# A hybrid decoder step on one core: first layer's result turned where it is made, low-rank rows from unmixed rows, second low-rank maps inside the dense loop, shared buffers

## The reference, cut to what matters

```
x_prev = rows shifted by one;  xx = x_prev - x;  xm = x + xx * mu      # six mixes: w a r k v g
r, k, v, g = [xr, xk, xv, xg] @ w_in[j]
w_log = -softplus(-(w0 + tanh(xw @ w1) @ w2)) - 0.5                   # w1: 1024x64, w2: 64x1024
decay = exp(-exp(w_log));   a = sigmoid(a0 + (xa @ a1) @ a2)
kk = k * k_k, normalised per head;   k = k * (1 + (a - 1) * k_a)
per token and head:  S = S * w + sa (kk * a)^T + v k^T;   o = S r      # 16 heads of 64x64
out = (groupnorm(o) + bonus) * silu(g);   y = LayerNorm(ALPHA * x1 + out @ w_out)
```

## Time and profile before

| | us |
|---|---|
| median of the runs | 2200.3 |
| profiled execution, its own time | 2204.67 |
| its span, first to last instruction | 2202.9 |
| PE busy / DVE busy / ACT busy / POOL busy | 1834.0 / 1237.6 / 576.1 / 401.4 |
| phase_gate_out | 880.2 to 1095.4 |
| phase_rwkv_in before its loop | 1095.4 to 1199.3 |
| its dense loop | 1199.3 to 1497.8 |
| its value, gate and inverse part | 1497.8 to 1780.2 |
| phase_wkv | 1780.2 to 2026.8 |
| phase_out | 2026.8 to 2202.9 |

### The profile page before, as it was taken

One profiled execution on the slowest core, in us unless ns is written; L12 is line 12 of the kernel. 1 busy time (PEld: TensorE's weight loads), 2 busy tenths in 40 slices (PEclk: granted clock), 3 DMA queues, 4 the chain that ended last, 5 costly groups with the idle time before them and its releaser, 6 DMA issues. The chain is left out here.

```text
span 2202.9 us, 30628 instructions
## 1 busy us (share of the span) xinstructions
PE 1834.0 (83%) x11638; PEld 1063.8 (48%) x11638; DVE 1237.6 (56%) x2382; ACT 576.1 (26%) x1153; POOL 401.4 (18%) x376
## 2 busy tenths in 40 slices
PE   8999466899993998799747999978989957774887
PEld 4445234444442687447233666653454436563432
DVE  2000064888998765473467667677534335563584
ACT  0000004500012553121145555561121114341100
POOL 0001110000013554110000333320003312323110
PEclk9999688999996999798877999988979978896999
DMA  4100724212301100831164344434757284863811
GB/s 179 72 34 33 190 92 137 77 38 72 115 34 71 37 21 10 322 113 44 57 134 173 106 140 143 145 122 98 137 130 152 82 211 118 205 152 94 265 68 39
DMA packets 276576, 245.65 MB, mean 112 GB/s; under 512 B 131996, under 2 KB 229308, under 8 KB 276172
## 3 DMA queue, kind: packets, MB, share of 16 engines
q1 hardware_dynamic: 272420, 232.64, 36.9%
q0 software_dynamic: 2976, 9.02, 1.2%
q10 hardware_dynamic: 1040, 2.10, 0.4%
HBM read 161.60 MB, written 86.63 MB: 113 GB/s over the span
## 5 line engine op out<-in xcount | busy, mean ns | idle before, releaser
L555 PE MATMUL ix_ps<-ix_src,ei_xT 128*128 128x512 f32 x512 | 223.9, 600 | 9.4 <-DMA ix_src<-in_e_w_in 9.4
L1794 PE MATMUL ri_ps<-ri_xm,ri_w 128*128 128x384 f32 (+1 forms) x768 | 231.3, 455 | 0.1
L1890 PE MATMUL ri_ps<-ri_w,ri_xm 128*128 128x512 f32 x512 | 226.7, 605 | 0.0
L186 PE MATMUL ei_ps<-ei_w,ei_xT 128*128 128x512 f32 (+1 forms) x432 | 188.5, 598 | 3.9 <-DMA ei_w<-in_e_w_in 3.9
L1794 PEld LDWEIGHTS ri_ps<-ri_xm,ri_w 128*128 128x128 f32 x768 | 144.2, 190 | 73.0 <-issue 0.8
L633 DVE TENSOR_SCALAR_CACHE_REDUCE ix_flags<-score,ix_cand 128x384 bf16<-128x384 f32 (+1 forms) x186 | 163.7, 942 | 12.2 <-DVE ix_cand L650 12.0
L555 PEld LDWEIGHTS ix_ps<-ix_src,ei_xT 128*128 128x128 f32 x512 | 98.0, 192 | 132.7 <-issue 123.1
L1890 PEld LDWEIGHTS ri_ps<-ri_w,ri_xm 128*128 128x128 f32 x512 | 99.3, 195 | 124.5 <-issue 124.4
L1386 PE MATMUL co_psm<-co_w,co_srcT 128*128 128x512 f32 (+1 forms) x288 | 130.1, 611 | 11.6 <-DVE co_y L1436 10.8
L1112 PE MATMUL go_psm<-go_w,go_srcT 128*128 128x512 f32 (+1 forms) x288 | 135.1, 629 | 4.7 <-DVE go_y L1254 4.4
L186 PEld LDWEIGHTS ei_ps<-ei_w,ei_xT 128*128 128x128 f32 (+1 forms) x432 | 77.6, 181 | 114.0 <-issue 114.0
(11 more groups left out here) (328 smaller groups left out, 3037.9 us busy)
## 6 DMA issues: line engine op xcount, KB each, us to landing
ix_src<-in_e_w_in SPq DMA_DIRECT2D x4, 2048.0 KB, 11.2
scratch_h<-ix_stage SPq DMA_DIRECT2D x32, 256.0 KB
ri_w<-in_c_w_in SPq DMA_DIRECT2D x16, 512.0 KB, 5.5
ri_w<-in_c_w_in SPq DMA_DIRECT2D x4, 2048.0 KB, 9.3
ei_w<-in_e_w_in SPq DMA_DIRECT2D x3, 2048.0 KB, 19.9
scratch_h<-ei_stage POOLq DMA_DIRECT2D x24, 256.0 KB, 2.3
ix_src<-scratch_h SPq DMA_DIRECT2D x3, 2048.0 KB, 9.2
go_uvg<-scratch_h SPq DMA_DIRECT2D x8, 768.0 KB, 10.9
```

What stands on the lines that cost most here:

```text
L186: last = nc.tensor.matmul(ps[n % NB][0:rows(t), 0:cw], xT[:, kd, t * P:t * P + rows(t)], rhs, start=(kd == 0), stop=(kd == KD - 1))
L555: last = nc.tensor.matmul(ps[n % NB][:], xT[:, kd, t * P:(t + 1) * P], w_rest[s % 2][:, kd], start=(kd == 0), stop=(kd == KD - 1))
L1794: last = nc.tensor.matmul(out[:, 0:wd], w[:, ct % 2, kd, i * P:(i + 1) * P], xm[:, i, kd, lo:lo + wd], start=(kd == 0), stop=(kd == KD - 1))
L1890: last = nc.tensor.matmul(out[:], xm[:, j, kd, t * P:(t + 1) * P], w[:, a, kd], start=(kd == 0), stop=(kd == KD - 1))
```

## The change

1. phase_gate_out turns its own result: `result(t)` puts 8 transposes of each finished tile (L1120) and ACT copies (L1203) into the buffer `rows_T`, which phase_rwkv_in reads as x transposed. The sample rows' V cache has half the buffer: four sequences are loaded when the sample bias has been added, the other four once the first values are done.
2. phase_rwkv_in loads its parameters as rows and turns them (L1853). The two first low-rank weights are scaled twice, with 1-mu and with mu (L2219 on DVE), and the hidden rows are made from unmixed rows and rows shifted by one (L1865, L1870). The mixes w and a are not formed. All scaling by 1-mu is on ACT.
3. The second low-rank maps (L1883) and their Sigmoids (L2027) are inside the dense loop, one item ahead, straight into the buffer that the loop reads; the DRAM copies `e` and `a` are gone.
4. Buffers are shared by the odd layer's phases (`Shared`). The first keys, reads and the constants of phase_wkv are loaded in the last part of phase_rwkv_in, and w_out and three input tiles of phase_out during phase_wkv.
5. In phase_wkv the state update is one DVE sum (L2661), with the decayed state SP made ahead (L2665); the output buffer has three slots, and the group-norm steps stand at other hops.
6. In phase_out the sample transposes (L1417) stand between tiles, the sample steps come three tiles later, and on SP the exchange of their vectors stands ahead of the first store of y.

The diff, cut to its core:

```diff
+            def result(t):
+                m = rows(t)
+                pe.wait_ge(y_d, t + 1)
+                for hf in range(2):
+                    bank(hf, "y", t)
+                    for j in range(4):
+                        kd = hf * 4 + j
+                        last = nc.tensor.transpose(ps_t[hf][:, j * P:j * P + m], y[0:m, t % 2, kd * P:(kd + 1) * P], ident[0:m, 0:m])
+                    last.then_inc(tr[hf], 1)
...
-            for s in range(NT + 3):
+            for s in range(NT + 5):
                 if s == LAST + 2:
                     project(LAST, 0)
-                if s >= 2:
+                if 2 <= s <= LAST + 2:
                     project(s - 2, 1)
+                if s >= 4:
+                    result(s - 4)
...
+            def result(t):
+                m = rows(t)
+                at = 1 + t * P
+                for hf in range(2):
+                    act.wait_ge(tr[hf], count[hf]["y", t])
+                    nc.scalar.copy(rows_T[:, hf * 4:hf * 4 + 4, at:at + m],
+                                   ps_t[hf][:].rearrange("p (j n) -> p j n", j=4)[:, :, 0:m]).then_inc(turned[hf], 1)
...
-            def load_ea(x):
-                ct, q = item(x)
-                lo, wd = PIECES[q]
-                sp.wait_ge(lo_out[x % 2], 32 * (x // 2 + 1))
-                for i, n in enumerate(("e", "a")):
-                    sp.dma_start(ea[:, x % 3, i, 0:wd], g[n][ct * P:(ct + 1) * P, lo:lo + wd]).then_inc(ea_in[x % 3], 16)
-
...
+            pe.wait_ge(w1_d, 4)
+            for q in range(2):
                 for kd in range(KD):
-                    for j in range(2):
-                        last = nc.tensor.matmul(ps[q][half(j), 0:wd], w1[:, j, kd], xm[:, j, kd, lo:lo + wd], start=(kd == 0), stop=(kd == KD - 1))
+                    for i, (m, at) in enumerate(((w1o, 1), (w1m, 0))):
+                        lo = q * AW + at
+                        last = nc.tensor.matmul(ps[4 + q][:], m[:, kd].rearrange("p i n -> p (i n)"), xT[:, kd, lo:lo + AW], start=(kd == 0 and i == 0), stop=(kd == KD - 1 and i == 1))
                 last.then_inc(hid_mm, 1)
+            pe.wait_ge(trc, 3)
+            for kd in range(KD):
+                for i, (m, x) in enumerate(((w1o, xs), (w1m, prv))):
+                    last = nc.tensor.matmul(ps[6][:, 0:DB], m[:, kd].rearrange("p i n -> p (i n)"), x[:, kd], start=(kd == 0 and i == 0), stop=(kd == KD - 1 and i == 1))
+            last.then_inc(hid_mm, 1)
             pe.wait_ge(hid_ev, 6)
-            for u in range(ITEMS):
-                ct, q = item(u)
+
+            def low_rank(x, j):
+
...
+                n = 2 * x + j
+                if n:
+                    pe.wait_ge(lo_ev, n)
+                if q == 0 and j == 0:
+                    pe.wait_ge(w2_in[ct % 2], 32 * (ct // 2 + 1))
+                nc.tensor.matmul(ps_lo[:, 0:wd], w2[half(j), ct % 2], hid[half(j), lo:lo + wd], start=True, stop=True).then_inc(lo_mm, 1)
...
+            low_rank(0, 0)
+            low_rank(0, 1)
             for x in range(ITEMS + 2):
                 y, z = x - 1, x - 2
                 if x < ITEMS:
                     ct, q = item(x)
+                    if x + 1 < ITEMS:
+                        low_rank(x + 1, 0)
                     if q == 0:
                         pe.wait_ge(wrk_in[ct % 2], 32 * (ct // 2 + 1))
...
                     wd = PIECES[item(y)[1]][1]
                     nc.tensor.matmul(ps_n[:, 0:wd], same[:], sq[:, 0:wd], start=True, stop=True).then_inc(n_mm, 1)
                 if x < ITEMS:
+                    if x + 1 < ITEMS:
+                        low_rank(x + 1, 1)
...
+            def low_rank(x, j):
+                ct, q = item(x)
                 wd = PIECES[q][1]
-                act.wait_ge(lo_mm, u + 1)
-                if u >= 2:
-                    act.wait_ge(lo_out[u % 2], 32 * (u // 2))
-                for i in range(2):
-                    nc.scalar.activation(lst[:, u % 2, i, 0:wd], ps[(2 * u + i) % NB][:, 0:wd], ACT.Sigmoid, bias=cols[:, i, ct:ct + 1]).then_inc(lo_ev, 1)
-
+                act.wait_ge(lo_mm, 2 * x + j + 1)
+                if x >= 3:
...
                     nc.scalar.activation(em[:, p, 0:n], cs[:, 0:n], ACT.Exp, scale=-DECAY).then_inc(em_d, 1)
+                    if x + 1 < ITEMS:
+                        low_rank(x + 1, 0)
                     act.wait_ge(csx_d, x + 1)
                     nc.scalar.activation(ex[:, p, 0:n], ex[:, p, 0:n], ACT.Exp, scale=DECAY).then_inc(ex_d, 1)
                     act.wait_ge(r_mm, x + 1)
@@ -1943,6 +2051,8 @@
                         act.wait_ge(prod_d, x - 1)
                         act.wait_ge(smp_d, 5 * ((x - 1) // 3))
                     nc.scalar.copy(r_sb[:, p, 0:wd], ps_r[p][:, 0:wd]).then_inc(r_ev, 1)
+                    if x + 1 < ITEMS:
+                        low_rank(x + 1, 1)
                 if 0 <= y < ITEMS:
...
+            step(nc.vector.tensor_scalar(omu[:], mu, -1.0, 1.0, ALU.mult, ALU.add), ready, 1)
+            dve.wait_ge(w1_in, 32)
+            for m, scale in ((w1o, omu), (w1m, mu)):
+                for i, j in enumerate((JW, JA)):
+                    nc.vector.tensor_tensor(m[:, :, i], w1[:, :, i], scale[:, j].unsqueeze(2).broadcast_to([P, KD, LORA]), ALU.mult).then_inc(w1_d, 1)
+            step(nc.vector.tensor_scalar(cols[:, 5], cols[:, 3], -1.0, 1.0, ALU.mult, ALU.add), ready, 2)
...
                 dve.wait_ge(s_mm, cc + 1)
                 if cc:
                     dve.wait_ge(o_mm, cc)
-                ch = cc % CHUNKS
-                for p in range(QP):
-                    nc.vector.scalar_tensor_tensor(S[:, (cc + 1) % 2, p], S[:, cc % 2, p], pcs[:, gr * QP + p, ch:ch + 1], ps_s[1 - cc % 2][:, p],
-                                                   ALU.mult, ALU.add).then_inc(S_d, 1)
+                nc.vector.tensor_tensor(S[:, (cc + 1) % 2], SP[:], ps_s[1 - cc % 2], ALU.add).then_inc(S_d, 1)
+                ch = cc % CHUNKS + 1
+                if ch < CHUNKS:
+                    dve.wait_ge(S_d, cc + 1)
+                    nc.vector.tensor_tensor(SP[:], S[:, (cc + 1) % 2], pcs[:, gr * QP:(gr + 1) * QP, ch:ch + 1].broadcast_to([P, QP, CL]), ALU.mult).then_inc(SP_d, 1)
                 for j in fill:
...
                     keep_r(j)
-                if n and k in (0, 2, 3):
-                    post(n - 1, {0: 0, 2: 1, 3: 2}[k])
+                if n and k == 0:
+                    post(n - 1, 0)
+                if n >= 2 and k == 1:
+                    post(n - 2, 2)
+                if n and k == 3:
+                    post(n - 1, 1)
...
+            load_src(sp, 3)
+            load_res(0)
+            sp.dma_start(gam, g["ln_g"][1].partition_broadcast(P)).then_inc(g_in, 16)
+            sp.dma_start(bet, g["ln_b"][1].partition_broadcast(P)).then_inc(g_in, 16)
+            side.loads(sp)
+            for t in range(1, NT + 1):
+                if 4 <= t + 3 < NT:
+                    load_src(sp, t + 3)
                 load_res(t)
+            sp.wait_ge(turned, at["s", 4] + 2)
+            side.exchange(sp)
             total = [0, 0]
             for t in tiles:
...
+    def exchange(self, sp):
+
+        g = self.g
+        sp.dma_start(g["vecs"].rearrange("q b d -> b q d"), self.tok).then_inc(self.vec_out, 16)
+        sp.wait_ge(self.vec_out, 16)
+        for i in range(5):
+            sp.dma_start(self.vec[:, i], g["vecs"][i].rearrange("b (h d) -> (b h) d", d=HD)).then_inc(self.vec_in, 16)
...
+            def load_first_keys():
+
+                sp.wait_ge(Dt_d, 2)
+                sp.wait_ge(D_out, 160)
+                for m in range(2):
+                    for name, buf in (("B", sh.B), ("K", sh.K)):
+                        sp.dma_start(buf[:, m], sh.by_channel(g, name, m)).then_inc(first_in, 16)
```

More of the change, by code:

```diff
@@ L998, in phase_gate_out @@
         LAST = NT
+        turns = [[("src", 0), ("src", 1)], []]
+        for s in range(1, NT + 5):
+            for hf in range(2):
+                if 0 <= s - 4 <= LAST:
+                    turns[hf].append(("y", s - 4))
+                t = s if 2 <= s < LAST else LAST if s == LAST + 1 else None
+                if hf == 0 and t is not None:
+                    turns[0].append(("src", t))
+                if hf == 1 and s - 1 <= LAST:
+                    turns[1].append(("src", s - 1))
+        count = [{item: n + 1 for n, item in enumerate(q)} for q in turns]
         tok = lambda ap, t: ap[t * P:t * P + rows(t)]
@@ L1147, in _, with turn @@
                     project(s - 1, 0)
+                if s == 7:
+                    side.values(pe, 4)
         @block.scalar
         def _(act):
-            def turned(t, hf):
+            def turn(t, hf):
                 m = rows(t)
-                act.wait_ge(tr[hf], t + 1)
+                act.wait_ge(tr[hf], count[hf]["src", t])
                 if t >= 2:
@@ L1465, in phase_rwkv_in @@
+def phase_rwkv_in(nc, g, sh):
     with ExitStack() as c:
@@ L2490, in _ @@
```

(10 more changed lines are left out.)

691 lines of the change are left out of this document (341 added, 350 removed).

## The result

The changed kernel takes 2255.1 us (median of four runs, 2253.3 to 2259.7) against 2201.8 for the kernel before on the same chip: ratio 1.0243, 95% interval 1.022 to 1.0267. It is slower by 53 us, where 20 were forecast; the range ended at 2246. Of the changed kernel's four executions the profiled one took 2259.7 us, the other three 2253.3 to 2255.7.

What follows compares the result with a forecast made beforehand. PE was taken to bound the dense loop, waits the other stretches; the change would make the loop chain-bound. Terms +5 - 54.2 + 99 + 0 - 25.4 - 4 = +20.4 us gave a predicted 2221 us, 8-in-10 range 2192 to 2246.

Steps and rivals of the forecast that it cites:

- Part 1: End of the even layer: turning the result costs PE 7.2 us, about half filling its wait for y; +5 us.
- Part 2: Stretch of phase_rwkv_in before the dense loop: new chain of 49.7 us in place of 103.9; -54.2 us.
- Part 3: Dense loop: three more table loads and two Sigmoids between scan and square root, a tile 33.9 to 47.2 us; +99 us.
- Part 4: Value and gate part: added loads and one POOL step run beside PE work; 0, or +5 us if a DMA is delayed.
- Part 5: phase_wkv: chunk products begin at once, -13.4 us, and shorter hops; -25.4 us together.
- The hops' -12: Hops of phase_wkv: taken as -12 us from a range of -20 to +4, with irregular issue waits and more loads beside them.
- -4 and -8: Hops of phase_wkv: gains in us from the state update as one sum and from moving the squares' idle time on ACT.
- Part 6: phase_out: earlier first projection and phase_wkv's tail, -16.6 us, against sample transposes and longer waits for y, +12.7; -4 us.
- the collision of LayerNorm with POOL's long step: Rival in phase_out: two more long DVE waits beside POOL's steps, +17 us, 2238; chance 0.18 shared with the half-clock rival.
- the loop hidden under PE: Rival in the dense loop: ACT's extra work falls into its waits, PE stays the bound, 2154 us; chance 0.07.
- the drain of 1.38 us: Rival in the dense loop: each table switch costs 2.66 us, 4.1 more an item, +95 us, 2316; chance 0.02.
- The slow clock: Rival in the dense loop: PE at half clock for a tenth of it, +24 us, 2245; chance 0.18 shared with phase_out's loss.

Runs made afterwards that it cites:

- experiment 1: Changed kernel with ACT's copies of the previous tile's turned result moved behind the normalisation in phase_gate_out; 2242.2 us, ratio 1.0171.
- experiment 4: Changed kernel with DVE's product for the decayed state placed behind the masking of the chunk products in phase_wkv; 2256.9 us, ratio 1.0249.
- Experiments 2 and 3: Each against the changed kernel: both Sigmoids moved behind the square root, 2206.1 us; each item's second Sigmoid replaced by a plain copy, one load fewer, 2233.6 us.
- Experiment 8: Kernel before with only the state update as one DVE sum, the decayed state made behind the masking; 2204.3 us, ratio 0.9996.
- experiment 10: Kernel with four queue-order moves together (2169.9 us), its group-norm squares on ACT put back where they were before; 2170.4 us, ratio 0.9849.
- experiment 5: Changed kernel with the stores of y's first two tiles ahead of the sample exchange on SP in phase_out; 2249.1 us, ratio 1.0202.

## Why the prediction was wrong

**Part 1 failed.** "Results of six tiles are turned before the last projection: 7.2", with half of it in PE's wait, priced the turns on PE alone: +5. On ACT their copies stand ahead of the normalisation that everything behind waits for, and I did not follow that queue. Measured +19.7 at the end of the layer; experiment 1 gives 16.4 of them to this one order. For the loop the prediction did follow ACT's queue; here it did not.

**Part 2** held: 45.0 us, forecast 49.7. The parameters were turned and w1 scaled by 1125.1, 10.0 us after the start (forecast 11.9), the 32 matmuls took 29.2 (28.3 + 1.5; no row stood behind the 1.5, and PE's clock was 0.50 in the first 3 us and 1.00 after), and the last steps were shorter than the sum had them.

**Part 3** held: a tile went from 33.9 to 47.4 us (forecast 47.2), the stage by 104.7 (99). Part of the rest lies at the loop's two ends, where the first intervals and the mixing steps lengthen too. Some 3.6 us go with the clock: from the fourth tile to the seventh the first item of a tile has a clock of 0.77, and the second takes 17.0 or 17.1 us. In experiment 4, with the same code in this stage, the clock of those first items is 0.88 or 1.00, the second items take 16.4, and the stage 682.0 us instead of 685.6. Experiments 2 and 3 show the cause of the rest: loads and Sigmoids in the chain between scan and square root, a load at about 1.3 us.

**Part 4**, 0, held: from the first value projection to phase_wkv it is 281.0 us before and 281.2 after.

**Part 5** was half right. PE's first matmul stands at the phase's start and the first X comes 13.3 us earlier, as forecast. The hops' -12 failed: they got 5.6 longer. "-4 and -8" took two waits out of a wait list as if nothing were behind them. Experiment 8 shows no gain for the first beyond the 2 us by which the kernel before itself scatters, because PE's waits for X and for itself take its place; experiment 10 has some 4 for the second. And the product ahead of the masking, which the prediction did not see, cost 6 to 9 in the traces (experiment 4). The loads beside the hops were not the 5.5 MB of the prediction's estimate there: 32.1 MB pass in them after the change and 30.6 before.

**Part 6** was right in its number for a reason that is half of it: PE waits 16.8 us for y, forecast 17. The held buffers were forecast; 8.5 of the 16.8 are the collision of LayerNorm with POOL's long step, which the prediction had as a rival of its own (experiment 5), so the 17 is in part luck. The first projection comes 3.5 us after the start (forecast 4.2). The phase is 5.0 us shorter, forecast 14.3 - 12.7 = 1.6, in the table 1.7 (the rest of part 6's 4 was phase_wkv's tail, which grew by 2.1 instead of shrinking by 2.3). Experiment 5 gives 7.5 us of the wait back.

The sum missed by 34.5: +14.7 in part 1, +17.6 in the hops, +4.4 in the tail, against -4.7, +5.7 and -3.3 in the others and 0.1 at the hops' start. The two steps that failed are thus the price of the turns, put on PE alone, and the gain in the hops, taken from single waits. Of the rivals, the loop hidden under PE and the drain of 1.38 us did not come. The slow clock came in a small part: 0.96 fell to 0.90 in the loop, and some 3.6 us go with it, where the rival had 24. The collision in phase_out came too, once on a step that PE waits for.

## What to carry to other kernels

A step that is added to an in-order queue is priced on every engine on which it issues something: ask what stands behind it there and how long its own input is away. A wait in a list is worth what is left once the next releaser is late, so take the gain from the difference between the two last ones, not from the list. Where a chain through several engines runs just under the bound, new activation functions belong outside it, next to each other: the same two Sigmoids cost 13.5 us a tile in the chain and, with two loads an item fewer, 5.2 beside it. A wait that comes out as forecast can still have another cause, so look up what stood in it.
